# Where an expert's weights lie: nine places for three pairs of experts, six in a loop, and a reordered last pair

## What is computed

```python
def expert_block(args):                    # xb: rows of one expert
    xb, e = args
    h = xb @ w_gate_up[e] + b_gate_up[e]   # 1024 x 2048
    g, u = h[:, :D_EXPERT], h[:, D_EXPERT:]
    g = jnp.minimum(g, SWIGLU_LIMIT)
    u = jnp.clip(u, -SWIGLU_LIMIT, SWIGLU_LIMIT)
    glu = g * jax.nn.sigmoid(g * SWIGLU_ALPHA)
    return ((u + 1.0) * glu) @ w_down[e] + b_down[e]   # 1024 x 1024
...
y = jnp.einsum('tkd,tk->td', ys[dest].reshape(T, TOP_K, D), gates)
x = layer_norm(DEEPNORM_ALPHA * x + y, ln3_g, ln3_b)
```

## Time and profile before

| what | us |
|---|---|
| median of three runs (lowest to highest) | 1226.02 (1224.87 to 1226.47) |
| the profiled execution, its own time | 1225.65 |
| its span, from first to last instruction | 1223.8 |
| PE, busy in the span | 1152.3 (94%) |
| DMA queue q1 (data), share of 16 engines | 86.6%, 439.96 MB |
| start of the first expert's matmuls | 291.40 |
| end of the last `down` | 1209.86 |

### The profile page before, as it was taken

How to read it: one execution, slowest core, us unless ns; L and a number is a source line. 1 busy time by engine, 2 the same in 40 slices (tenths; PEclk the granted TensorE clock), 3 DMA queues, 4 the chain that set the end, 5 groups by cost and what they waited for, 6 DMA issues and landing times.

```text
span 1223.8 us, 13031 instructions
## 1 busy us (share of the span) xinstructions
PE 1152.3 (94%) x5372; PEld 523.7 (43%) x5372; DVE 219.8 (18%) x552; ACT 133.9 (11%) x288; POOL 48.6 (4%) x59
## 2 busy tenths in 40 slices
PE   9999999999999999999899999898989789998985
PEld 7686746754334343433333443333333324342421
DVE  1223112124211111121111211111111111111113
ACT  2133101221000000000000100000000000000002
POOL 0032003210000000000000000000000000000000
PEclk9999999999999999999999999999999989999999
DMA  9943333386999999999999999999999999999993
GB/s 357 314 157 138 125 122 140 130 341 242 428 415 427 428 428 429 428 427 427 428 427 427 428 427 429 428 428 426 428 428 427 427 427 427 428 428 428 428 428 121
DMA packets 54391, 445.93 MB, mean 364 GB/s; under 512 B 10136, under 2 KB 11296, under 8 KB 29760
## 3 DMA queue, kind: packets, MB, share of 16 engines
q1 hardware_dynamic: 52032, 439.96, 86.6%
q10 hardware_dynamic: 2304, 5.12, 1.2%
HBM read 444.01 MB, written 1.06 MB: 364 GB/s over the span
## 4 chain that ended last, share of the span: by engine, by line
PE 67%; DMA 28%; DVE 2%; issue 2%; ACT 1%; POOL 0%; SPq 0%; DVEq 0%
PE bank L1527 21%; DMA ring<-in_w_gate_up 18%; PE bank L1548 13%; DMA reg_kv<-in_w_gate_up 9%; PE bank L1187 9%; PE bank L1174 9%; PE bank L1426 5%; PE bank L1487 2%; PE bank L1502 2%; PE bank L1537 1%; PE bank L1371 1%; PE bank L1205 1%; DMA ring<-in_w_in 1%; DVE reg_k L1085 1%; DVE reg_k L1082 0%
## 5 line engine op out<-in xcount | busy, mean ns | idle before, releaser
L1527 PE MATMUL bank<-ring,PT 128*64 128x512 f32 x1392 | 309.7, 596 | 25.9 <-DMA ring<-in_w_gate_up 18.2
L1527 PEld LDWEIGHTS bank<-ring,PT 128*64 128x64 f32 x1392 | 98.3, 137 | 231.9 <-issue 194.3
L1548 PE MATMUL bank<-ring,NCt 128*64 128x512 f32 x672 | 148.8, 595 | 0.7 <-ACT NCt L717 0.7
L1174 PE MATMUL bank<-reg_bc,ring 128*128 128x256 f32 x480 | 106.7, 381 | 1.8 <-ACT reg_bc L642 1.8
L1077 DVE TENSOR_SCALAR reg_k<-bank 128x512 f32<-128x512 f32 x32 | 22.1, 692 | 465.9 <-PE bank L1527 465.9
L708 ACT ACTIVATE reg_v<-reg_k 128x512 f32<-128x512 f32 x32 | 20.2, 630 | 744.4 <-DVE reg_k L1077 744.4
L1174 PEld LDWEIGHTS bank<-reg_bc,ring 128*128 128x128 f32 x480 | 90.3, 190 | 16.6 <-issue 4.8
L1548 PEld LDWEIGHTS bank<-ring,NCt 128*64 128x64 f32 x672 | 46.4, 137 | 100.0 <-issue 91.5
L1527 PE MATMUL bank<-reg_kv,PT 128*64 128x512 f32 x336 | 75.9, 594 | 5.7 <-DMA reg_kv<-in_w_gate_up 5.7
L1094 DVE COPY reg_v<-bank 128x512 f32<-128x512 f32 x32 | 22.1, 692 | 304.3 <-PE bank L1548 304.3
L1426 PEld LDWEIGHTS bank<-L,reg_a 128*128 128x128 f32 x512 | 62.9, 196 | 24.8 <-issue 23.5
(11 more groups left out here) (215 smaller groups left out, 681.3 us busy)
## 6 DMA issues: line engine op xcount, KB each, us to landing
ring<-in_w_gate_up SPq DMA_DIRECT2D x87, 2048.0 KB, 34.7
ring<-in_w_down SPq DMA_DIRECT2D x42, 2048.0 KB, 38.3
reg_kv<-in_w_gate_up SPq DMA_DIRECT2D x21, 2048.0 KB, 36.8
reg_q<-in_w_down SPq DMA_DIRECT2D x11, 2048.0 KB, 35.2
reg_bc<-in_w_down SPq DMA_DIRECT2D x11, 2048.0 KB, 36.6
reg_q<-in_w_gate_up SPq DMA_DIRECT2D x10, 2048.0 KB, 31.7
reg_bc<-in_w_gate_up SPq DMA_DIRECT2D x10, 2048.0 KB, 33.2
ring<-in_w_in SPq DMA_DIRECT2D x5, 2048.0 KB, 17.5
```

The source lines that it names most:

```text
L1174: last = mm(B(name)[:, a * T:(a + 1) * T], w[:, k, c:c + P], src[:, k, :], start=(k == 0), stop=(k == KD - 1))
L1527: last = mm(ps[half * CAP:(half + 1) * CAP, :], xgT[:, k, i * CAP:(i + 1) * CAP], w[:, j, col:col + HALF], start=False, stop=(k == KD - 1) ...
L1548: last = mm(xy_ps[half * CAP:(half + 1) * CAP, :], hT[:, a:a + CAP], w[:, j, half * HALF:(half + 1) * HALF], start=(k == 0), stop=(k == KD ...
```

## The change

- Places by number: pairs 0 to 2 still go round nine places. From expert 6 on, chunk c of an expert always goes to place c, so six places are used, and chunk c of expert e is issued when chunk c of expert e-1 has been used. PE's code for a pair is then always the same: PE has three pairs written out, a loop with one pair in its body for pairs 3 to 5, pair 6 with `base` written out, a loop for pairs 7 to 14 and the last pair, `final_pair`. SP's loop has one expert in its body.
- Half a place more at the start: `reg_k` takes row 0 of chunk 0 of expert 0 (`lent`, 1 MB), and place 0 takes row 1 of it and row 0 of chunk 9. The matmuls of the very first `gate_up` go over k in the order 1, 0, 2, 3. DVE writes the first `Sg` only after the lent row has been used.
- The first two places are released by halves: the other half of chunk 9 is issued after one k, the first half of chunk 10 after three and its second half after four.
- The last pair: both gate and up first, then `down` of expert 30 (with the transposes of expert 31 between its chunks), then `down` of expert 31 into another bank, `tr_ps`; its hidden rows lie in `hT_last`. Expert 31's chunks 0 to 2 go to places 6 to 8 (`FINAL`), transfers are in the order of use, and the very last chunk comes in pieces of two, one and one rows. Tile 1 of expert 30's scatter stands behind the last `down`.

```diff
+OPEN = 2 * NSLOT // CH
+RINGED = OPEN * 2 * CH // NSLOT - OPEN * 2
+FINAL = {(0, 0): 0, (0, 1): 1, (0, 2): 2, (0, 3): 3, (1, 0): 6, (1, 1): 7, (1, 2): 8, (1, 3): 4,
+         (0, 4): 5, (0, 5): 0, (1, 4): 1, (1, 5): 2}
+PIECES = [(0, 2), (2, 3), (3, 4)]
...
+                if n == 0:
+                    load_row(0, 0, 1, 0)
+                    sp.dma_start(slot_tile(NSLOT, 3)[:, 0:1, :], chunk_source(1, 3)[:, 0:1, :]).then_inc(ahead_in, 16)
+                    continue
+                if n == NSLOT - 1:
+                    sp.dma_start(lent, chunk_source(0, 0)[:, 0:1, :]).then_inc(lent_in, 16)
                 load_chunk(n // CH, n % CH, n)
...
-            for n in range(NSLOT, 3 * CH):
-                reload(n // CH, n // CH, n % CH)
-            with sp.Fori(1, NE // 3) as t:
-                for u in range(3):
-                    for c in range(CH):
-                        reload(t * 3 + u, u, c)
+            sp.wait_ge(opened, 1)
+            load_row(1, 3, 1, NSLOT)
+            rows = DNJ // 2
+            sp.wait_ge(opened, 2)
+            sp.dma_start(slot_tile(NSLOT + 1, 4)[:, 0:rows, :], chunk_source(1, 4)[:, 0:rows, :]).then_inc(ahead2_in, 16)
+            wait_used(1, 1)
+            sp.dma_start(slot_tile(NSLOT + 1, 4)[:, rows:, :], chunk_source(1, 4)[:, rows:, :]).then_inc(slot_in[1], 16)
+            for n in range(NSLOT + 2, OPEN * 2 * CH):
+                wait_used((n - NSLOT) % CH, (n - NSLOT) // CH + 1)
+                load_chunk(n // CH, n % CH, n)
+            for c in range(CH):
+                n = OPEN * 2 * CH - NSLOT + c
+                wait_used(n % CH, n // CH + 1)
+                load_chunk(OPEN * 2, c, c)
+            with sp.Fori(OPEN * 2 + 1, NE - 2) as e:
                 for c in range(CH):
-                    reload(e, e % 3, c)
+                    wait_used(c, e)
+                    load_chunk(e, c, c)
+            for c in range(GUC):
+                wait_used(c, NE - 2)
+                load_chunk(NE - 2, c, FINAL[0, c])
+            for c in range(GUC - 1):
+                load_chunk(NE - 1, c, FINAL[1, c])
+            wait_used(4, NE - 2)
+            load_chunk(NE - 1, 3, FINAL[1, 3])
...
+            for piece, (j0, j1) in zip(piece_in, PIECES):
+                sp.dma_start(slot_tile(n, c)[:, j0:j1, :], chunk_source(e, c)[:, j0:j1, :]).then_inc(piece, 16)
...
-            places(Sg, 0, True).then_inc(sg_ready, 1)
...
+            dve.wait_ge(chunks_used, 1)
+            places(Sg, 0, True).then_inc(sg_ready, 1)
...
+            def final_pair(p):
+                gate_up(p, 0, "final")
+                pe.wait_ge(y_sb, p * 2)
+                scattered(1)
...
+                gate_up(p, 1, "final")
+                pe.wait_ge(sgT_sb, p + 1)
+                pe.wait_ge(hT_sb, p * 2 + 1)
+                final_down(p, 0, xy_ps, hT, lambda: transpose_h(p * 2 + 2))
+                pe.wait_ge(y_sb, p * 2 + 1)
+                scattered(0, tiles=(0,))
+                pe.wait_ge(hT_sb, p * 2 + 2)
+                final_down(p, 1, tr_ps, hT_last)
+                scattered(0, tiles=(1,))
...
-            for p in range(BASE_PAIR + 3):
-                pair(p, p // 3, p % 3, first=p == 0, with_base=p == BASE_PAIR)
-            with pe.Fori(BASE_PAIR // 3 + 1, NE // 6) as t:
-                for u in range(3):
-                    pair(t * 3 + u, t, u)
-            pair(NE // 2 - 1, NE // 6, 0, last=True)
+            for p in range(OPEN):
+                pair(p, "open")
+            with pe.Fori(OPEN, BASE_PAIR) as p:
+                pair(p, "loop")
+            pair(BASE_PAIR, "loop", with_base=True)
+            with pe.Fori(BASE_PAIR + 1, NE // 2 - 1) as p:
+                pair(p, "loop")
+            final_pair(NE // 2 - 1)
```

More of the change, by code:

```diff
@@ L264, in hybrid_layer @@
         hT = NCt[:, :, :].rearrange("p a b -> p (a b)")[:, 0:512]
+        hT_last = PT[:, 0, :]
         bgu = after[:, 1536:2048]
@@ L404, in hybrid_layer @@
         far = [reg_q[:, :], reg_bc[:, :, :, :].rearrange("p a k t -> p (a k t)"), reg_kv[:, :]]
+        lent = reg_k[:, :].rearrange("p (j n) -> p j n", j=1)
         def slot_tile(n, c):
@@ L716, in pair @@
                     act.wait_ge(hT_done, p * 2 + (i + 1))
-                    nc.scalar.activation(hT, tr_ps[:, :], ACT.Copy).then_inc(hT_sb, 1)
+                    nc.scalar.activation(hT_last if last and i == 1 else hT, tr_ps[:, :], ACT.Copy).then_inc(hT_sb, 1)
             pair(0)
@@ L1098, in _ @@
             pair(BASE_PAIR, with_base=True)
-            with dve.Fori(BASE_PAIR + 1, NE // 2) as p:
+            with dve.Fori(BASE_PAIR + 1, NE // 2 - 1) as p:
                 pair(p)
+            p = NE // 2 - 1
+            for i in range(2):
+                swiglu(p, i)
+            places(S, p + 1, False).then_inc(s_ready, 1)
+            places(Sg, p + 1, True).then_inc(sg_ready, 1)
+            for i, ps in enumerate((xy_ps, tr_ps)):
+                dve.wait_ge(y_done, p * 2 + i + 1)
+                nc.vector.tensor_copy(ysb[:, i, :], ps[:, :]).then_inc(y_sb, 1)
             extra = dve.value_load(ctl[0:1, MAXX:MAXX + 1], min_val=0, max_val=MAXX // 2)
@@ L1480, in base, with scatter @@
                    start=True, stop=True).then_inc(over_done, 1)
-            def scatter(i, opens=False):
-                for tt in range(TT):
+            def scatter(i, opens=False, tiles=range(TT)):
+                for tt in tiles:
                     for half in range(2):
@@ L1489, in scatter, with scattered @@
                     yield last
-            def scattered(i, opens=False):
-                for _ in scatter(i, opens):
+            def scattered(i, opens=False, tiles=range(TT)):
+                for _ in scatter(i, opens, tiles):
                     pass
@@ L1502, in biases, with chunk, gate_up @@
                     mm(ps[:, :], bsel[rows, i, :], bgu[rows, :], start=True, stop=False, skip_group_check=True)
[L1504 to L1514, removed]
+            def chunk(p, i, c, stage):
+                if stage == "open":
+                    n = (p * 2 + i) * CH + c
+                    loads = n // NSLOT + 1
+                elif stage == "loop":
+                    n, loads = c, p * 2 + (i + 1 + RINGED)
+                elif stage == "final":
+                    n = FINAL[i, c]
+                    loads = OPEN * 2 * CH // NSLOT + 1
+                    if n < CH:
+                        loads += NE - 2 - OPEN * 2 + ((i, c) in ((0, 5), (1, 4)))
+                else:
+                    n, loads = c, p * 2 + (i + 1 + RINGED + (1 if c < 2 else 0) - 1)
+                pe.wait_ge(slot_in[n % NSLOT], loads * 16)
+                return slot_tile(n, c)
+            def gate_up(p, i, stage):
                 if i == 0:
                     pe.wait_ge(xgTa_sb, p + 1)
-                for k in range(KD):
+                opening = stage == "open" and type(p) is int and p == 0
+                for n, k in enumerate([1, 0] + list(range(2, KD)) if opening and i == 0 else range(KD)):
                     if i == 0 and k == KD // 2:
@@ L1521, in gate_up @@
                     c, j = k // GUJ, k % GUJ
-                    if j == 0:
-                        w = chunk(turn, u, i, c)
+                    if n % GUJ == 0:
+                        w = chunk(p, i, c, stage)
+                        if opening and (i, c) == (1, 3):
+                            pe.wait_ge(ahead_in, 16)
+                    if opening and (i, k) == (0, 0):
+                        pe.wait_ge(lent_in, 16)
+                        w = lent
                     for ps, c0 in ((gate_ps, 0), (up_ps, F)):
@@ L1528, in gate_up @@
                                       w[:, j, col:col + HALF], start=False, stop=(k == KD - 1), skip_group_check=True)
-                    if j == GUJ - 1 and k < KD - 1:
+                    if opening and (i, n) in ((0, 0), (0, 2)):
+                        last.then_inc(opened, 1)
+                    elif n % GUJ == GUJ - 1 and k < KD - 1:
                         last.then_inc(chunks_used, 1)
@@ L1538, in transpose_h, with down @@
                 last.then_inc(hT_done, 1)
-            def down(i, turn, u):
+            def down(p, i, stage):
                 for k in range(KD):
@@ L1544, in down @@
                     if j == 0:
-                        w = chunk(turn, u, i, c)
+                        w = chunk(p, i, c, stage)
+                        if stage == "open" and (p, i, c) == (0, 1, 4):
+                            pe.wait_ge(ahead2_in, 16)
                     a = (k % 4) * P + (k // 4) * CAP
@@ L1553, in down, with final_down @@
                     last.then_inc(y_done, 1)
-            def pair(p, turn, u, first=False, with_base=False, last=False):
-                gate_up(p, 0, turn, u)
+            def final_down(p, i, ps, h, between=None):
+                for k in range(KD):
+                    c, j = GUC + k // DNJ, k % DNJ
+                    if (i, c) != (1, CH - 1):
+                        if j == 0:
```

(51 more changed lines are left out.)

43 lines of the change are left out of this document (27 added, 16 removed).

## The result

The changed kernel takes **1220.11 us** (median of 6 runs, 1217.82 to 1220.39), the kernel before beside it 1225.58 (6 runs, 1224.87 to 1226.54): a ratio of 0.995, 95% interval 0.9938 to 0.9961, faster by 5.5 us. Forecast were 1219.6. The profiled execution of after took 1219.53 with a span of 1217.7, so 6.1 of span against the one before, where the sum said 6.4. But the sum came out by luck: two of its terms were wrong by 2.0 to 2.5 us, in opposite directions, and cancel.

The account below looks back on a forecast made before the run. The weight stream was taken to bound the kernel, PE having time to spare. Start -2.0, loops -4.6, tail 0 and small rows +0.2 summed to -6.4, forecast 1219.6 us; own range 1217 to 1222, 8 in 10 1216.5 to 1228.

Parts of the forecast that it names:

- What bounds the kernel: Whole span: weights stream without a pause for three quarters of it; PE has 4.83 us to spare in each pair.
- Six places for nine: Weight places from expert 6 on: fewer places cost 0, bound 2 us if two tight spots are missed.
- The loops, 4.6: PE's pair loops: repeated passes fetch no instructions, 21 packets fewer, three stream steps of 1.53 gone, 4.6 us less.
- The start, 2.0: First pair: lent row and places released by halves restart the stream earlier, 2.0 us less (bounds 0 and 3.1).
- The tail, 0: Last pair: reordering gains 0, as PE's jump over the code for further experts binds (bounds -0.7 and +0.5).
- -2.5 if jump did not bind: Last pair: bound of 2.5 us less if PE's jump over the further experts' code did not set the scatter.
- last scatter 6 to 7.5 after the last landing: End of kernel: a sign that the forecast is right, last scatter starting 6 to 7.5 us after the last weights land.
- Small rows, +0.2: Last chunk's pieces: rows of 4 KB may run slower, 0.2 us more.
- DVE's `Sg`, 0: First pair: DVE's first `Sg`, moved to after 294.9, delays nothing wanted earlier, 0 us.
- refetch at each jump: PE's loops: each jump back fetches its instructions again and costs only the fetch, 1227.5 us; chance 0.20.
- PE as the bound: PE's loops: each jump back costs 9.5 us as the old one did, so PE decides, 1260 us; chance 0.06.
- six places short: At the change to six places or in pair 6 the queue runs dry by 2 to 4 us, 1222.5; chance 0.09.

Follow-up runs that it names:

- half dose: The changed kernel with idle POOL running 128 empty instructions at each of 24 places: 1231.52 us, ratio 1.0044.
- written-out loops: The changed kernel with PE's two loops of one pair written out, all else kept: 1222.96 us, ratio 0.9967 to the kernel before.
- old last pair: The changed kernel with the last pair in the order of before, six places to the end and the last chunk whole: 1221.82 us, ratio 0.9960.
- jump behind: The changed kernel with PE's jump over the code for further experts put after tile 1's last scatter: 1218.11 us, ratio 0.9931.
- third place: The changed kernel with PE's jump put after the last scatter and also chunk 13 loaded by halves: 1218.19 us, ratio 0.9935.
- two pairs: The changed kernel with two pairs instead of one in the body of PE's second loop: 1219.13 us, ratio 0.9948.
- control: The changed kernel run again as it is, as the measure for other runs on its chip: 1219.74 us, ratio 0.9948 to the kernel before.
- old start: The changed kernel with the start of before, no row lent and chunks 9 and 10 whole: 1220.71 us, ratio 0.9954.
- full dose: The changed kernel with idle POOL running 256 empty instructions at each of 24 places, 6144 in all: 1247.98 us, ratio 1.0178.

## Why the prediction was right, and where it was not

- **What bounds the kernel:** right. All that was won or lost in the ten kernels is found in the last landing or behind it. Six places for nine cost nothing (no digit of 8 in the DMA row from the eleventh slice on, and chunks land 4.9 apart where the loops begin). The row was misread in one place: the low digits of before are the third to the eighth slice, with 8 and 6 behind them, and not the fifth to the ninth. Nothing hung on it.
- **The loops, 4.6:** the mechanism is right and shown from both sides: writing the loops out brings back the packets and the steps, packets of another engine make steps of their own. The steps fell away as counted, but the one that stayed was not the one at 534.3: after has its at 666.2 and 691.4. PE holds the head of its loop; q8 is at 26 where 27 were forecast. What spoke for it in advance was weak, though: the packet at 704.7 on q14, read as DVE's, stands on the queue that carries POOL's packets too (half dose), so it isn't shown to be DVE's, nor that DVE's loop crosses a border. PE's own runs decide it. In the profiled executions the term is 4.6; by medians and ratios it is 2.1 to 3.2 for the new loops and up to 1.2 for the old jump, 2 to 4 together.
- **The start, 2.0:** this is the step that failed. "I take 2.0" rested on chunk 11's earlier landing, which came (2.4), and on chunk 13's limit at 316.5, which was named. What was not priced is that PE's clock can drop in the pause behind the first `swiglu`, which moved chunk 13's issue from 313.76 to 315.11, and that the most delayed DMA engine need not share the gain. The drop is not all of it: in the six kernels with the new start and no drop (the written-out loops, the old last pair, the jump behind, the third place, the two pairs and the half dose) chunk 22 landed 0.1 to 1.3 before the kernel before's 371.24, in the three with the drop 0.4 to 2.0 behind it. So even undisturbed the start brings less than the 2.0. Undone, it costs 0.5 to 1.0 us, not told from nothing. (A k of 13.9 / 8 is 1.74, not 1.72; the halves were released when forecast all the same.)
- **The tail, 0:** a term that was mis-sized. The mechanism was right (PE gets to its condition at the last landing, 1200.44 against 1200.38, and its jump and not the copy sets the scatter). But the jump took 3.74 where 4.72 was carried over, and the rest of that stretch was at the lower end: 4.93 from the condition to the scatter instead of 6.0. The bound "-2.5 if jump did not bind" had the right sign and fell short: with the jump behind the scatter it was 3.7 (3.23 against 6.95). So the sign "last scatter 6 to 7.5 after the last landing" did not come.
- **Small rows, +0.2:** the three pieces of the last chunk landed 4.94 after the chunk before, where a whole chunk takes 4.89: 0.05. DVE's `Sg`, 0: right.
- **The rivals:** refetch at each jump, PE as the bound and six places short are all excluded by after's rows. The place that carried the doubt, whether PE keeps its loop's head, was the right one to doubt.

**Open:** why the clock dropped in the first pair in some executions (after, control, the old start and, for 6.8 us, the full dose) and not in others (before and the other seven). No run changed that alone. Nor is it shown which transfer delays the one engine between chunks 13 and 22; one of PE's packets and the loads of ln3 and `b_down` fall there. And it is open how much of the start's gain would last without the drop: one profiled execution of each kernel is too little for that.

## What to carry to other kernels

When weights stream without a pause, count the packets of instructions, and not only the weights: each delays one DMA engine by more than its bytes, and a tile has landed only when its last engine has. A loop short enough that the engine keeps its head (here 4.15 packets on PE) fetches nothing, and long straight code on an idle engine is not free. And a jump over code that is seldom run belongs behind the last work of the ordinary case: that was 2 us, as much as a reordered last pair. Before a saving at the start is counted, follow it to a late landing, and not only to the first chunks: here 2.4 at chunk 11 were gone at chunk 22.

## What the runs showed of the hardware

- A packet of PE's (16 KB) delayed its DMA engine by 1.5 us, one of POOL's (8 KB) by 0.66. Of the weights an engine carries 131 KB in 4.89 us, so that 8 KB would be 0.3 and 16 KB 0.6: by this estimate a packet of PE's costs 2.5 times its bytes and one of POOL's 2.2 times.
- By the marks, PE's packets go over eight DMA engines in turn (one step in about eight packets), POOL's over one and the same (one mark 14.2 behind the other fifteen).
- PE refetches nothing with bodies of 2.06 and 4.15 packets; with 6.2 it did, 6.4 us at the branch. The taken jump forward at the end took 4.7 in before and 3.7 in after, each with a packet fetched while it lasted.
- The granted clock of PE fell to 0.57 in a window of 4 us behind a pause of 2.4 us of waiting for DVE in one execution, and stayed at 1.00 in another (before) with the same pause.
